# Moving the last mixer's attention stages inside the product groups, and splitting the second rows' transposes differently, in a two-block transformer kernel on one core

## The reference

```python
q, k, v, z = jnp.split(h @ w_in, 4, axis=-1)
q = rms_norm(heads(q), q_gain) * (HEAD_DIM ** -0.5)
k = rms_norm(heads(k), k_gain)
s_own = jnp.einsum('hqd,hkd->hqk', qc, k_own)            # causal, minus slope * distance
p = jax.nn.softmax(scores, axis=-1)
out = jnp.einsum('hqk,hkd->hqd', p_own, v_own)
y = out * jax.nn.silu(z)
return h + y @ w_out
```

## Time and profile before

| | |
|---|---|
| time, median of 3 runs | 1410.7 us |
| the profiled execution, its own time | 1412.48 us |
| span of that execution | 1410.7 us |
| PE busy | 1389.1 us, 98% |
| DVE busy | 845.5 us, 60% |
| ACT busy | 728.6 us, 52% |
| POOL busy | 66.3 us, 5% |
| DMA | 251.41 MB, mean 178 GB/s |
| mean granted TensorE clock | 0.996 |

### The profile page before, as it was taken

The page is one execution under the profiler, slowest core; times in us unless marked ns, Lnnn a source line. Parts: engine busy times, 40 slices in busy tenths (PEclk is TensorE's granted clock), DMA queues, the critical chain, the costliest instruction groups (busy, mean ns, idle before and its releaser), DMA issues. The chain is left out here.

```text
span 1410.7 us, 19001 instructions
## 1 busy us (share of the span) xinstructions
PE 1389.1 (98%) x6458; PEld 1143.5 (81%) x6458; DVE 845.5 (60%) x1066; ACT 728.6 (52%) x1026; POOL 66.3 (5%) x117
## 2 busy tenths in 40 slices
PE   8999999999999999999999999999999999999998
PEld 6888888888888888878888888878888878888776
DVE  6555766666665555575555554575555675577665
ACT  5444454444454445474444455664444565555683
POOL 1000010000010000010000000010000110002000
PEclk9999999999999999999999999999999999999998
DMA  7656545555645666446567554455666455545431
GB/s 241 190 185 207 183 158 190 180 190 192 201 139 188 194 207 219 153 148 212 178 197 236 164 179 135 135 164 178 188 214 231 143 180 193 182 152 174 147 120 61
DMA packets 186525, 251.41 MB, mean 178 GB/s; under 512 B 15540, under 2 KB 115420, under 8 KB 186460
## 3 DMA queue, kind: packets, MB, share of 16 engines
q1 hardware_dynamic: 186172, 250.43, 55.0%
q10 hardware_dynamic: 288, 0.13, 0.0%
HBM read 249.45 MB, written 1.05 MB: 178 GB/s over the span
## 5 line engine op out<-in xcount | busy, mean ns | idle before, releaser
L1392 DVE TENSOR_TENSOR w_lo<-raw,w_hi 128x1024 fp32r<-128x1024 f32 x460 | 539.6, 1220 | 181.8 <-ACT w_hi L980 180.7
L980 ACT ACTIVATE w_hi<-raw 128x1024 fp32r<-128x1024 f32 x460 | 460.6, 1051 | 135.4 <-PE sums L499 66.9
L497 PE MATMUL sums<-w_hi,x_hi 128*128 128x512 f32 x1312 | 522.4, 398 | 4.8 <-DVE x_lo L1411 3.7
L499 PE MATMUL sums<-w_hi,x_lo 128*128 128x512 f32 x1312 | 512.4, 391 | 0.0
L498 PE MATMUL sums<-w_lo,x_hi 128*128 128x512 f32 x1312 | 511.5, 390 | 0.0
L497 PEld LDWEIGHTS sums<-w_hi,x_hi 128*128 128x128 f32 x1312 | 246.9, 188 | 58.3 <-issue 9.9
L499 PEld LDWEIGHTS sums<-w_hi,x_lo 128*128 128x128 f32 x1312 | 246.5, 188 | 52.1
L498 PEld LDWEIGHTS sums<-w_lo,x_hi 128*128 128x128 f32 x1312 | 247.2, 188 | 49.2 <-issue 1.0
L497 PE MATMUL sums<-w_hi,y_hi 128*128 128x512 f32 x512 | 202.0, 395 | 0.0
L498 PE MATMUL sums<-w_lo,y_hi 128*128 128x512 f32 x512 | 200.0, 391 | 0.0
L499 PE MATMUL sums<-w_hi,y_lo 128*128 128x512 f32 x512 | 200.0, 391 | 0.0
(11 more groups left out here) (171 smaller groups left out, 780.9 us busy)
## 6 DMA issues: line engine op xcount, KB each, us to landing
raw<-in_ffn_w_gate_dram SPq DMA_DIRECT2D x176, 256.0 KB, 3.9
raw<-in_ffn_w_up_dram SPq DMA_DIRECT2D x176, 256.0 KB, 4.8
raw<-in_ffn_w_down_dram SPq DMA_DIRECT2D x176, 256.0 KB, 3.9
raw<-in_ret_w_in_dram SPq DMA_DIRECT2D x96, 256.0 KB, 4.0
raw<-in_conv_w_in_dram SPq DMA_DIRECT2D x64, 256.0 KB, 4.0
raw<-in_attn_w_in_dram SPq DMA_DIRECT2D x64, 256.0 KB, 3.9
raw<-in_sb_w_in_dram SPq DMA_DIRECT2D x48, 256.0 KB, 3.6
raw<-in_ret_w_out_dram SPq DMA_DIRECT2D x32, 256.0 KB, 4.5
```

What stands on the lines that cost most here:

```text
L497: pe.matmul(bank[:, :], a, wh, start=(first and c == 0), stop=False, skip_group_check=True)
L499: mm = pe.matmul(bank[:, :], b, wh, start=False, stop=(last and c == SC - 1), skip_group_check=True)
L980: act.activation(w_hi[:, n % RING].rearrange("p c n -> p (c n)"), raw[:, n % RAW].rearrange("p c n -> p (c n)"), ACT.Copy).then_inc(hi_mad ...
L1392: dve.tensor_tensor(w_lo[:, n % RING].rearrange("p c n -> p (c n)"), raw[:, n % RAW].rearrange("p c n -> p (c n)"), w_hi[:, n % RING].rear ...
```

## The change

There are five edits.

- The transposes of the t = 1 rows: at ordinary boundaries the first part moves from behind step 1 to the middle of step 2 (behind its first chunk; `products` gets a `between`), the second stays behind step 2. At b = 4 and 8 they go behind steps 2 and 3.
- VectorE's `x_part` for t = 1 makes `xg` and `x_lo` of the first half of the width, then of the second. At the start of the program (b = 0, t = 0) the `w_lo` of slot 0 goes between the `xg` and the `x_lo`.
- ScalarE makes `w_hi` of two slots fewer before the second rows at b = 0 (4 instead of 6).
- On TensorE stage k of the last mixer, for k = 0 to 7, moves from behind group 8 + k into it, behind step 1; `mb_turn(1, 1)` from inside group 10 to behind group 9. On ScalarE stage m - 8 stands before the copy of group m. 
- The first rows for `moba_out`: `mb_turn_y(0, 0)` stays behind group 15, now with stage 7 ahead of it. `mb_y_hi(0, 0)` goes behind the copy of group 15, `mb_y_lo(0, 0)` behind stage 7. `mb_turn_y(0, 1)` moves behind stage 8 and a part of slot 1, and the waits of the PSUM bank follow.

```diff
-            def products(bank, t, n, j, c0, hi, lo, first, last, sign):
+            def products(bank, t, n, j, c0, hi, lo, first, last, sign, between=None):
...
+                    if between and c == 0:
+                        between()
...
-                return {1: lambda: turn_h(b, 1, [0]), 2: lambda: turn_h(b, 1, [1])}
+                if boundaries[b].startswith("ple"):
+                    return {2: lambda: turn_h(b, 1, [0]), 3: lambda: turn_h(b, 1, [1])}
+                return {(2, 0): lambda: turn_h(b, 1, [0]), 2: lambda: turn_h(b, 1, [1])}
...
-                if hd in (13, 15):
-                    pe.wait_ge(y_lo_made, y_base("moba") + (1 if hd == 13 else 2))
+                if hd == 15:
+                    pe.wait_ge(y_lo_made, y_base("moba") + 1)
...
-                if (half, i) != (1, 1):
-                    pe.wait_ge(mb["pt_flat"], 12 + 2 * (2 * half + i))
+                if (half, i) == (0, 0):
+                    pe.wait_ge(mb["pt_flat"], 14)
+                elif (half, i) != (1, 1):
+                    pe.wait_ge(mb["pt_flat"], 16)
...
-            hooks = {3: lambda: mb_turn(0, 0), 5: lambda: mb_turn(1, 0), 7: lambda: mb_turn(0, 1),
-                     15: lambda: (mb_turn_y(0, 0), mb_stage(7))}
-            hooks.update({8 + k: lambda k=k: mb_stage(k) for k in range(7)})
-            in_proj("moba_in", 9, hooks, {10: {2: lambda: mb_turn(1, 1)}})
+            hooks = {3: lambda: mb_turn(0, 0), 5: lambda: mb_turn(1, 0), 7: lambda: mb_turn(0, 1), 9: lambda: mb_turn(1, 1),
+                     15: lambda: mb_turn_y(0, 0)}
+            in_proj("moba_in", 9, hooks, {8 + k: {1: lambda k=k: mb_stage(k)} for k in range(8)})
...
-                     {0: lambda: (mb_turn_y(0, 1), mb_stage(8)), 1: lambda: mb_stage(9),
+                     {0: lambda: mb_stage(8), (1, 0): lambda: mb_turn_y(0, 1), 1: lambda: mb_stage(9),
...
-                split_to(ph.slot0 + 6)
+                split_to(ph.slot0 + (6 if b else 4))
                 x_part(b, 1)
...
-                if m == 15:
-                    mb_y_hi(0, 0)
+                if m >= 8:
+                    mb_stage(m - 8)
                 copy_rows(ph, m, dst, ACT.Silu if i == 3 else ACT.Copy)
...
                 if m >= 8:
-                    mb_stage(m - 8)
                     if m == 9:
                         mb_flat(1, 1)
+                    if m == 15:
+                        mb_y_hi(0, 0)
                     split_to(min(ph.slot0 + 24 + 2 * (m - 8), SLOTS - 4))
+            mb_stage(8)
             mb_y_hi(0, 1)
-            mb_stage(8)
...
-            def x_part(b, t):
+            def x_part(b, t, between=None):
...
+                if t == 0:
+                    scaled(0)
+                    scaled(1)
+                    if between:
+                        between()
+                    low(0)
+                    low(1)
+                else:
+                    scaled(0)
+                    low(0)
+                    scaled(1)
+                    low(1)
...
-            x_part(0, 0)
+            x_part(0, 0, lambda: split_to(1))
...
             for k in range(8):
+                mb_stage(k)
                 if k == 7:
                     mb_y_lo(0, 0)
-                mb_stage(k)
                 if k == 5:
                     mb_gate(0)
                 split_to(min(s0 + 24 + 2 * k, SLOTS - 4))
+            mb_stage(8)
             mb_y_lo(0, 1)
-            mb_stage(8)
```

More of the change, by code:

```diff
@@ L522, in group @@
                     sign = sums_done if last else (slot_used if t == 1 else None)
-                    products(sums[(ph.group0 + m) % BANKS], t, n, j, SC * s, hi, lo, s == 0, last, sign)
+                    products(sums[(ph.group0 + m) % BANKS], t, n, j, SC * s, hi, lo, s == 0, last, sign, hooks.get((s, 0)))
                     if s in hooks:
@@ L1399, in split_to, with scaled @@
                     split_next[0] += 1
-            def x_part(b, t):
+            def x_part(b, t, between=None):
                 gain = pre_gain[boundaries[b]]
-                for q in range(2):
+                def scaled(q):
                     dve.wait_ge(h_turned, 4 * b + 2 * t + q + 1)
@@ L1408, in x_part, with low @@
                                       gain[:, 4 * q:4 * q + 4].unsqueeze(2).to_broadcast([P, 4, P]), ALU.mult).then_inc(xg_made, 1)
-                for q in range(2):
+                def low(q):
                     dve.wait_ge(x_hi_made, 4 * b + 2 * t + q + 1)
```

## The result

The changed kernel takes **1423.4 us** (median of 4 runs, 1423.04 to 1423.52) against 1410.9 us before (4 runs beside it): ratio 1.0088, 95% interval 1.0075 to 1.0100, slower by 12.5 us. The forecast was 1420.4 (1411.5 to 1426.0), slower with 0.83. The profiled execution after took 1423.04 us (span 1421.2), 10.6 more than the profiled one before; the forecast for that difference was 9.7. The medians differ by 2 more.

The account below looks back on a forecast made before the run. TensorE, busy 1389.1 of 1410.7 us, was taken as the bound. 1412.5 - 4.4 - 2.5 - 2.2 + 2.4 + 16.4 = 1422.2, on the median's scale 1420.4 us; range 1411.5 to 1426.

Parts of the forecast that it names:

- the last mixer's term: Last mixer to the last addition: copies and table loads lengthen the VectorE-ScalarE cycle, costing 16.4 us (bounds 4.5 to 19).
- Start: Program start, b = 0: group 1 begins at 17.67 instead of 20.39, at full clock; gain 4.4 us.
- Ordinary boundaries: b = 1, 2, 5, 6: group 1 begins at 208.98 instead of 209.61; gain 0.6 us each, 2.5 for four.
- b = 4 and 8: Boundaries behind a gate phase: step 2 fills the wait for h; gain 1.05 and 1.15 us, 2.2 together.
- Gate phases: b = 3, 7: the new x_part order delays w_hi and w_lo; cost 1.2 us each, 2.4 together.
- The ring: Last mixer's VectorE-ScalarE cycle; T(k) starts VectorE's first L1832 of stage k; steps 8.70 (v), 11.28 (z) against TensorE's 8.48.
- Stage 1: Last mixer: TensorE's transposes wait for T(0) with steps 2 and 3 of group 9 still to do; 3.5 us lost.
- The end: moba_out: first y_hi product, behind stage 7's exponentials, load and copy, at 1393.7; last addition at 1423.3.
- Rival 3: Last mixer: TensorE's stalls lower the clock and feed the ring; up to 3 to 5 us more, 1424.5; chance 0.14.
- (1): Last mixer: the copy hides in a wait, every T step at most 8.48; 1408.5 us, not slower; chance 0.10.
- (2): Last mixer: table loads overlap with a wait, T(7) 9.0 earlier; 1411.4 us; chance 0.06.
- (4): Last mixer: each table switch also costs the Trainium skill's drain of about 1380 ns; 1430.1 us; chance 0.01.

Follow-up runs that it names:

- e2: The kernel before with the change's last-mixer edits alone, boundary edits left out: 1427.1 us, ratio 1.0111 to the kernel before.
- e5: The kernel before with the boundary edits alone, but the old x_part order at gate phases b = 3 and 7: 1404.2 us, ratio 0.9951.
- e4: The changed kernel with z copied without Silu in the last mixer, leaving out that silu: 1412.7 us, ratio 1.0011.
- e9: e6 with ScalarE's copy of group m ahead of stage m - 8 as before, TensorE's stages still inside the groups: 1416.7 us, ratio 1.0037.
- e6: The changed kernel with y_hi(0, 0) ahead of stage 7's exponentials and y_lo(0, 0) ahead of its first L1853: 1415.4 us, ratio 1.0027.
- e3: The changed kernel with ScalarE's two w_hi ahead of the copy of group m, except m = 9: 1418.7 us, ratio 1.0053.
- e12: e10 with ScalarE's wait for VectorE's gate moved from the copies of groups 14 and 15 to behind stage 5: 1410.6 us, ratio 0.9992.
- e10: e9 with the edits of e5 (old x_part order in gate phases) and e7 (w_lo inside the last norm): 1413.0 us, ratio 1.0009.
- e7: e5 with VectorE's w_lo of two slots made inside mb_norm(1, 1), in its wait for GpSimd: 1402.8 us, ratio 0.9941.
- e8: e7 with first-row y_hi, y_lo pairs right behind stages 6 and 7 and the last w_hi, w_lo pair behind them: 1401.7 us, ratio 0.9929.
- e11: The kernel before with the edits of the program's start (b = 0) alone: 1408.4 us, ratio 0.9976.

## Why the prediction was right

The direction, the mechanism and nearly all terms held. The time was 3.0 above the forecast of 1420.4, for two reasons. One is the last mixer's term, below. The other is the step from the profiled execution's scale to the median's: the absolute forecast for the changed kernel was 1422.2, and 1423.0 was measured in its profiled execution. Taking 1.8 off it had no ground: the four executions of the changed kernel lie at 1423.0 to 1423.5, the profiled one has no slow start to lose (1.00 in that window), and the slow start of before had been counted already, as 1.7 of the gain at the start.

- **Start**: 4.4 forecast (2.7 and 1.7 for the clock), 4.51 in the trace (3.03 at group 1, and 1.48 behind it). That the sum came so near is in part luck. The clock's share is a matter of the execution: e2, with before's code, had no slow stretch there and was 0.63 earlier at group 1 and 2.12 at group 2.
- **Ordinary boundaries**: 0.6 each forecast, 0.66 to 0.69 measured. **b = 4 and 8**: 1.05 and 1.15 forecast, 1.03 and 1.19. **Gate phases**: a cost of 1.2 each forecast, 1.19 and 1.21, and e5 gives it back. Together -6.7 forecast, -6.98 measured at the start of the last mixer's phase.
- **The ring**: v steps 8.70 forecast, 8.67; z steps 11.28 forecast (its four addends make 11.26), 11.38. The 0.10 is at the second load. It starts at 1361.17, when the accumulator read that ends the last exponential is over (1360.97 and 0.19 long); `w_hi`, which stood there before, started 0.09 ahead of such an end.
- **Stage 1**: 5.4 of waits were forecast, 2.8 measured (2.23, 0.36 and 0.21), but behind the first of them the clock was at 1.2 GHz. TensorE lost 5.2 there (a shift of -7.31 ahead of it, -2.08 at group 11), where 3.5 was forecast. It did not matter: TensorE next waits for the ring in stage 5, at 1361.21.
- **The end**: with the 6.98 of earlier gains added back, T(0) was 1317.34 (forecast 1317.15), T(7) 1386.06 (1385.7), the first product with `y_hi` 1394.36 (1393.7), and the last addition, at 1417.51 in this row of VectorE, 1424.49 (1423.3):

```profile
1417.51 0.69 DVE L1786 TENSOR_TENSOR h<-sums,h 128x512 f32<-128x512 f32 x1 [0.67 <-PE sums L499]
```

The term that was mis-sized is the last mixer: 16.4 forecast, 17.6 measured (from -6.98 to +10.58). Of the 1.2 missing, 0.36 had come by T(7), 0.3 between T(7) and the product, and 0.5 behind it. There the clock was down for twelve products, against eight in the kernel before; at 0.2 us each that is 0.8, and the forecast had 0.4. Rival 3 had that in it, but its feedback into the ring did not happen: the step from stage 1 to 2, behind the stretch at 1.2 GHz, is 9.83, and 9.85 was forecast without a feedback (8.70 + 1.15).

- **The other rivals**: no slack in the ring (1): the steps of 11.38 rule it out. The loads do not leave it (2): e4 is 10.7 faster without them. No drain (4): behind a load of 1.28 the activation starts after 0.01, 1359.06 in the fence above, and the load itself starts 0.03 or less behind the instruction before it, which disagrees with the Trainium skill (ScalarE: Activation LUTs, What ACT_TABLE_LOAD costs) on the drain and agrees on the load.
- **What it did not see**: why ScalarE's copy had to move at all. The prediction priced the copy's new place; e9 shows that the old place costs as much once TensorE's stages stand inside the groups, because the copy waits for a group that contains the stage.

What stays open: how much TensorE's place costs by itself with an order on ScalarE that fits it best (each copy as late as its reader allows). With the copy first (e9), behind the exponentials (e6) and last (e3) the kernel is slower than before each time.

## What to carry to other kernels

Where two engines hand work back and forth, write the cycle down as a sum of instructions and compare it with the third engine's pitch; whatever is put inside the cycle costs its full length once the sum is over the pitch, whatever the busy shares say. Before moving a producer inside a loop body, look in the consumer's in-order queue for the instruction that waits for the end of that body: it stands ahead of what you meant to bring forward. And put the split that the bound engine waits for ahead of work that only feeds later stages: that one order was worth 8 of the 12 us here (e6).

## What the runs showed of the hardware

A table load of 1.28 us hides in the wait of its activation where that has one wait (1346.19 in e9, copy at 1349.07) and stands behind the wait where there were two (1376.55 in e9, copy at 1377.84). With the second wait moved away, the load started right behind the instruction before it (e12), worth 1.6 us in the traces. That the first of two waits becomes an instruction of its own, which holds back the load too, is inferred from the records.

A GpSimd operation on 128x16 values that takes 0.20 us by itself took 1.10, 1.11 and 1.25 (e10, e7, e12) when it started while VectorE subtracted a `w_lo` of 128x1024, and the power behind it took 3.75 and 3.92 instead of 2.90 (e10, e12) when it started beside a second `w_lo`. In e8 the subtraction began 0.3 after the first operation had ended, beside the power, and both kept their 0.20 and 2.90. That the start waits for VectorE is inferred from these records; no run was made for it.

The clock's fall differs between executions of the same code: the kernel before ran its start at 0.71 in the profiled execution, while e2, with the same start, ran it at 1.00 and reached group 2 2.1 us earlier. Of the 22 executions of the kernel before beside e11, thirteen have a mean granted clock of 0.996 and took 1411.9 to 1413.3 us, and nine have 0.997 and took 1409.9 to 1411.5, but for one of 1412.5. Where they lost it is on record for the profiled one alone. A gain read from one profiled execution there (4.3 in e11's trace) was 3.6 in the medians (2.1 to 4.7).
